# Sparse experts with one token per partition: choices fetched as blocks, value rows added by VectorE

## The chip, the core and the metric

The kernel runs on one core of a Trainium2 chip. Its time is the device time of one execution in microseconds; the time of a kernel is the median of its runs.

## The reference, cut to what matters

One decoder layer for 512 prompt tokens and 32 sample tokens (8 sequences of 4), D = 1024. The change is in its last part, the PEER channel mixer, in which each of 8 heads chooses 16 of 16384 experts for each token:

```python
s = jnp.einsum('tpcd,pckd->tpck', q, peer_keys)          # two halves of 128 keys per head
s1, i1 = lax.top_k(s[:, :, 0], P_TOPK)                   # 16 of 128, twice
s2, i2 = lax.top_k(s[:, :, 1], P_TOPK)
cand = (s1[..., :, None] + s2[..., None, :]).reshape(P_TBLOCK, P_HEADS, P_TOPK * P_TOPK)
cidx = (i1[..., :, None] * P_NKEYS + i2[..., None, :]).reshape(...)
top_s, j = lax.top_k(cand, P_TOPK)
eidx = jnp.take_along_axis(cidx, j, axis=-1)             # 8 x 16 = 128 experts per token
gate = jax.nn.softmax(top_s, axis=-1)
u, v = peer_u[eidx], peer_v[eidx]                        # rows of 1024
act = jax.nn.gelu(jnp.einsum('td,tpkd->tpk', xb, u))
return jnp.einsum('tpk,tpkd->td', gate * act, v)
```

After it `y = layer_norm(DN_ALPHA * h + peer_ffn(h))`.

## The kernel before, in words

Everything ahead of `stage_peer` (projections, mLSTM, attention, merge, first norm) ends near 1087 us and isn't touched. Engines run their own programs and meet at semaphores. In `stage_peer` there are four parts.

- Queries and key scores, 1087 to 1229 us. TensorE projects the queries (L2284) and multiplies them with the keys (`score`, L2191), 4 groups of 4 score blocks for 5 token tiles (4 of 128 prompt tokens, one of 32 samples). ScalarE copies them to `sc`. VectorE ranks them (`top_two`, 16 of 128 per block) and, for every second group, combines two rankings (`choose`, L2444 to L2475) into 16 experts per head.
- The tokens are handled in two ways. The first 384 (tiles 0 to 2, `TD`) are computed densely, against all 16384 experts. The other 160 (tile 3 and the samples, `TG`) are computed sparsely, with their 128 rows of `peer_u` and `peer_v` fetched.
- Hidden stage, 1229 to 1945.6 us. The loop runs over `NCH` = 128 chunks of 128 experts. `hidden(n)` on TensorE is 8 x 2 matmuls of the high part `u_hi` with both parts of h (L2216, L2217) and 8 of the low part `u_lo` (L2227), each over 384 tokens. SyncE loads `u_raw` (4 buffers), ScalarE makes `u_hi` (`high`), and `u_lo` is made by GpSimd (`low`, L2144) up to chunk 47 and from 119, by VectorE (L2517) between. ScalarE applies the gelu, SyncE stores it to HBM. From chunk 47 to 104 the gate tables are made: VectorE writes two one-hots per 4 tokens (`one_hots`, L2483), ScalarE scales one (`scaled`), TensorE multiplies them (`gate_table`, L2247, 96 of them), ScalarE copies the result (`gate_copy`), and SyncE writes it out in 48 pieces of 512 KB.
- Sparse dots lie in the same loop, from chunk 49 to 117. For one token i GpSimd gathers the 128 rows of `peer_u` that it chose (`gather`, L2137; the choices stand in the partitions, a row of 4 KB in each), TensorE copies the token's h to all partitions (`row_spread`, L2203, two matmuls over 512 columns), and VectorE multiplies and sums (`sparse_dot`, L2492). There are 160 of each, six row buffers.
- Output stage, 1945.6 to 2578 us. 32 groups of 4 expert columns. GpSimd loads the value rows of a group (`load_v`, 2 MB, two buffers), SyncE the gate table and the gelus (768 KB each), VectorE multiplies them (`weigh`, L2503), ScalarE makes the high parts (`v_high`, `w_high`), VectorE the low parts (`v_lo` L2508, `w_lo` L2511). `out_tile` (L2270) is 6 matmuls over 512 columns for one column and one of 3 token tiles. After every third column TensorE does `sparse_out` (L2261): 4 tokens' gathered value rows, with the weights as a stationary tile of 32 columns, 40 times in all. Before `load_v(g)` GpSimd issues the gathers of `sparse_rows` in turn. At the end VectorE normalizes the tiles.

The order of the work around the change is written out by hand: `rows_due(n)` and `quads(n)` say what each engine does in chunk n, and each queue is in program order.

Of the kernel before, what the change touches and what calls it, by code (L numbers as in the profile page):

```python
# [8 lines left out]
ALU = mybir.AluOpType  # L9
ACT = mybir.ActivationFunctionType  # L10
AX = mybir.AxisListType
# [1899 lines left out]
def stage_peer(nc, s, io):  # L1911
# [8 lines left out]
    SG = 3  # L1920
    i128 = at("i128", 9136, [P, PK])
# [7 lines left out]
    sc = at("key_scores", 24368, [P, NT, 4 * SG, PK])  # L1929
# [7 lines left out]
    oh = at("oh", 37744, [P, 2, HC * TOPK, TOPK])  # L1937
    chosen = at("chosen", 39792, [P, 3, T])
    picks = [(h0, t) for h0 in range(0, PH, HC) for t in range(NT)]
# [5 lines left out]
    gas = at("gelu_out", 9648, [P, 2, 2, TD])  # L1945
# [8 lines left out]
    row_at = [11184, 12208, 22192, 23216, 49616, 34608]  # L1954
    GR = len(row_at)
    grow = [at(f"gathered{i}", row_at[i], [P, D]) for i in range(GR)]
    hb_at = [7088, 8112, 36656]
    hb_raw = [at(f"h_pair_raw{i}", hb_at[i], [P, D]) for i in range(3)]
    hb = [at(f"h_pair{i}", hb_at[i], [P, D], F32R) for i in range(3)]
    hb_hi = [at(f"h_pair_hi{i}", [49616, 50640, 37680][i], [P, D], F32R) for i in range(3)]  # L1960
    sel = at("pick_row", 13232, [P, 64], F32R)
    wzb = at("sparse_wz", 32560, [P, 4, 4, 64])
    hid = at("sparse_hid", 33584, [P, TG])
    gls = at("sparse_gelu", 33744, [P, TG])
    idx = at("sparse_idx", 33904, [P, TG], U32)
    wsp = at("sparse_w", 34064, [P, TG])
    srow_at = [49616, 12720, 52176, 34608, 5040, 6064, 47568, 48592]
    srow = [at(f"sparse_row{i}", srow_at[i], [P, D]) for i in range(8)]
    hs = at("h_s", 35632, [P, D])
    gb = at("ln2_gb", 7088, [P, 2, D])  # L1970
# [5 lines left out]
    whi = [at(f"w_hi{i}", [50640, 41424][i], [P, GJ, TD], F32R) for i in range(2)]  # L1976
    wlo = [at(f"w_lo{i}", [36656, 42960][i], [P, GJ, TD], F32R) for i in range(2)]
    gin = [at(f"gelu_in{i}", [11184, 44496][i], [P, GJ, TD]) for i in range(2)]
    gt = [at(f"e_gate{i}", [22192, 46032][i], [P, TD, GJ]) for i in range(2)]
    wt = at("e_w", 38704, [P, 2, TD])  # L1980
    hr = at("h2", 944, [P, 4, D])
    st = at("ln2_st", 34232, [P, 2, 6])
    mv = at("ln2_mv", 34248, [P, 2])
    rs = at("ln2_rs", 34256, [P, 2])

    NCH = PK
    E_AT, R_AT, G_AT, G_LEN = 45, 46, 47, 58
    S_AT, S_LEN, HB_AT, HS_AT, SL_AT = 49, 68, 60, 68, 118
    L_AT, W_AT, YS_AT, YP_AT = 119, 121, 26, 122

    due = [S_AT + i * S_LEN / TG for i in range(TG)]
    NSG = TG // 4
    NSS = TS // 4

    def rows_due(n):

        return [i for i in range(TG) if n <= due[i] < n + 1]

    def row_in_group(k, g):

        return P + 4 * k + g if k < NSS else 32 * g + k - NSS

    v_v = io.peer_v.rearrange("(a b) d -> a b d", a=PK)
    sem = Semaphores(nc)
    with ExitStack() as ctx:
# [9 lines left out]
        ul_end = sem("u_low_end")  # L2015
        uh_done, ul_done, ul_late, h_psum, gelu_done = sem("u_high_done"), sem("u_low_done"), sem("u_low_late"), sem("eh_psum"), sem("gelu_done")
# [5 lines left out]
        idx_ready = sem("idx_ready")  # L2022
        row_in = [sem(f"row_in{i}") for i in range(GR)]
        hb_in, hb_split, hb_ready, hb_psum = sem("hb_in"), sem("hb_split"), sem("hb_ready"), sem("hb_psum")
        hid_done, gls_done, wz_zero, sp_read = sem("hid_done"), sem("gls_done"), sem("wz_zero"), sem("sp_read")
        hs_zero, hs_in, gb_in = sem("hs_zero"), sem("hs_in"), sem("ln2_gb_in")
        srow_in = [sem(f"srow_in{i}") for i in range(8)]
        wsp_ready, wzb_ready, sv_psum = sem("wsp_ready"), sem("wzb_ready"), sem("sv_psum")
# [10 lines left out]
        def quads(n):  # L2039
            lo, hi = (min(max((m - G_AT) * NQD // G_LEN, 0), NQD) for m in (n, n + 1))  # L2040
            return range(lo, hi)

        def pieces(n):

            first = [next(m for m in range(NCH) if QD * b + QD - 1 in quads(m)) for b in range(NTB)]
            return [(b, n - first[b]) for b in range(NTB) if 0 <= n - first[b] < NPIECE]

        last_tiles = (3, 0, 1, 2)

        @block.sync  # L2050
        def _(sp):
# [4 lines left out]
            def load_rows(i):  # L2056

                n = 64 if i < 2 else TS
                t0 = TD + 64 * i
                for p0 in range(0, P, n):  # L2060
                    sp.dma_start(hb_raw[i][p0:p0 + n, :], io.h_rows[t0:t0 + n, :]).then_inc(hb_in, 16)

            for n in range(UB):
                load_u(n)
            load_rows(0)
            load_rows(1)
# [4 lines left out]
            for n in range(NCH):  # L2071
# [3 lines left out]
                if n % 2:  # L2075
                    sp.wait_ge(gelu_done, n + 1)
                    c = n % GJ - 1
                    sp.dma_start(io.gelus[n // GJ, :, c * TD:(c + 2) * TD], gas[:, n // 2 % 2, :, :].rearrange("p c t -> p (c t)"))\
                      .then_inc(ga_sent[n // 2 % 2], 16)
                if n == R_AT:  # L2080
                    sp.wait_ge(topk_done, 1)
                    load_rows(2)
# [701 lines left out]
```

## Time and profile before

| | us |
|---|---|
| median of 3 runs | 2606.28 (2597.03 to 2609.4) |
| the profiled execution | 2593.42 |
| its span, first to last instruction | 2591.7 |
| TensorE busy (page, part 1) | 2409.0 (93%) |
| VectorE busy | 1472.6 (57%) |
| ScalarE busy | 897.4 (35%) |
| GpSimd busy | 673.1 (26%) |
| DMA, mean over the span | 200 GB/s |

The page's engines are PE (TensorE matmul), PEld (its weight loads), DVE (VectorE), ACT (ScalarE), POOL (GpSimd) and SP (SyncE). A busy time is an average over stages with different limits, so the rows are read stage by stage. Matmul times in the groups overlap each other, so TensorE's price of a step is read from the chain of waits or from start to start in the timeline.

### The profile page before, as it was taken

How to read it: one execution, taken by the hardware profiler on the slowest of the kernel's cores; microseconds unless marked ns; L12 is line 12 of the kernel's file. 1: busy time of each engine (PE TensorE's matmuls, PEld its weight loads, DVE VectorE, ACT ScalarE, POOL GpSimd, SP SyncE). 2: the span in 40 equal slices, each digit the busy share in tenths (PEclk: the TensorE clock that was granted, in tenths of full speed). 3: DMA queues.
4: the chain of work that ended last, by engine and by line, in shares of the span. 5: the costliest groups of instructions: out<-in, count | busy, mean ns of one | idle time of the engine just before them, and what ended most of it. 6: DMA issues, size and time to landing. Idle time of an engine off the chain costs nothing.

```text
span 2591.7 us, 36634 instructions
## 1 busy us (share of the span) xinstructions
PE 2409.0 (93%) x14200; PEld 2015.6 (78%) x14200; DVE 1472.6 (57%) x3408; ACT 897.4 (35%) x1780; POOL 673.1 (26%) x549
## 2 busy tenths in 40 slices
PE   6999899878977798899999999999999999999997
PEld 6898877765545695488999899999996767777775
DVE  3344332317762332359999888888743454545546
ACT  2122222206841321122333666666332233323321
POOL 0001232211200000100666444444453333233220
PEclk8999999968986699999999999999999999999998
DMA  5234323330012133420555899999989888888881
GB/s 178 80 137 120 108 82 106 119 109 1 1 66 66 50 137 127 150 66 17 165 171 168 275 325 361 354 344 353 374 338 360 315 328 331 327 341 340 322 336 65
DMA packets 160485, 519.25 MB, mean 200 GB/s; under 512 B 15365, under 2 KB 52345, under 8 KB 155577
## 3 DMA queue, kind: packets, MB, share of 16 engines
q1 hardware_dynamic: 104856, 265.27, 30.0%
q0 software_dynamic: 55456, 251.64, 25.9%
q8 instruction: 114, 1.87, 0.3%
q14 instruction: 59, 0.48, 0.1%
HBM read 447.23 MB, written 73.75 MB: 201 GB/s over the span
## 4 chain that ended last, share of the span: by engine, by line
PE 39%; DVE 12%; DMA 3%; issue 3%; POOL 1%; ACT 1%; DVEq 0%; POOLq 0%
PE ps_e L2270 16%; PE ps_e L2216 4%; PE ps_e L2217 4%; PE ps_e L2227 4%; PE ps_e L2247 3%; PE ps_e L2203 3%; PE ps_e L2284 2%; PE ps_e L2261 2%; DMA v_raw<-in_peer_v 2%; DVE oh L2473 2%; DMA u_raw<-in_peer_uT 1%; DVE idx L1898 1%; DVE idx L1902 1%; DVE oh L2468 1%; DVE res L2475 1%
## 5 line engine op out<-in xcount | busy, mean ns | idle before, releaser
L2216 PE MATMUL ps_e<-hTh,u_hi 128*128 128x384 f32 x1024 | 347.2, 339 | 0.0
L2217 PE MATMUL ps_e<-hTl,u_hi 128*128 128x384 f32 x1024 | 346.6, 338 | 0.0
L2508 DVE TENSOR_TENSOR v_lo<-v_raw,v_hi 128x1024 fp32r<-128x1024 f32 x128 | 157.8, 1233 | 292.2 <-ACT v_hi L2349 270.5
L2137 POOL DMA_INDIRECT gathered<-in_peer_u,sparse_idx x160 | 206.5, 1291 | 255.0 <-DVE sparse_hid L2492 238.7
L2137 POOL DMA_INDIRECT sparse_row<-in_peer_v,sparse_idx x160 | 173.1, 1082 | 356.6 <-PE ps_e L2261 312.6
L2270 PE MATMUL ps_e<-v_hi,w_hi 128*128 128x512 f32 x768 | 247.9, 404 | 9.6 <-DVE w_lo L2511 9.6
L2270 PE MATMUL ps_e<-v_lo,w_hi 128*128 128x512 f32 x768 | 242.4, 397 | 0.0
L2349 ACT CAST v_hi<-v_raw 128x1024 fp32r<-128x1024 f32 x128 | 134.4, 1050 | 309.5 <-DMA v_raw<-in_peer_v 309.5
L2270 PE MATMUL ps_e<-v_hi,w_lo 128*128 128x512 f32 x768 | 241.3, 395 | 0.0
L2492 DVE CUSTOM_DVE_ANT_0 gathered<-gathered,ps_e 128x1024 f32<-128x1024 f32 x160 | 193.0, 1218 | 40.2 <-PE ps_e L2203 38.6
L2144 POOL TENSOR_TENSOR u_lo<-u_raw,u_hi 128x1024 fp32r<-128x1024 f32 x57 | 149.2, 2622 | 228.9 <-ACT u_hi L2323 228.9
L2227 PE MATMUL ps_e<-hTh,u_lo 128*128 128x384 f32 x1024 | 200.7, 338 | 0.0
L2270 PEld LDWEIGHTS ps_e<-v_hi,w_hi 128*128 128x128 f32 x768 | 142.0, 189 | 75.2 <-issue 31.9
L2216 PEld LDWEIGHTS ps_e<-hTh,u_hi 128*128 128x128 f32 x1024 | 192.9, 188 | 5.9 <-issue 0.2
L2217 PEld LDWEIGHTS ps_e<-hTl,u_hi 128*128 128x128 f32 x1024 | 192.9, 188 | 5.6
L2227 PEld LDWEIGHTS ps_e<-hTh,u_lo 128*128 128x128 f32 x1024 | 181.8, 188 | 2.0
L238 PE MATMUL ps_proj<-xT_hi,w_hi 128*128 128x256 f32 (+2 forms) x528 | 153.9, 292 | 21.5 <-DVE w_lo L301 13.8
L2270 PEld LDWEIGHTS ps_e<-v_lo,w_hi 128*128 128x128 f32 x768 | 145.6, 190 | 35.0
L2270 PEld LDWEIGHTS ps_e<-v_hi,w_lo 128*128 128x128 f32 x768 | 145.1, 189 | 34.5
L2323 ACT CAST u_hi<-u_raw 128x1024 fp32r<-128x1024 f32 x128 | 134.4, 1050 | 73.7 <-DMA u_raw<-in_peer_uT 73.6
L239 PE MATMUL ps_proj<-xT_lo,w_hi 128*128 128x256 f32 (+2 forms) x528 | 154.2, 292 | 0.0
L240 PE MATMUL ps_proj<-xT_hi,w_lo 128*128 128x256 f32 (+2 forms) x528 | 153.8, 291 | 0.0
(477 smaller groups left out, 4827.3 us busy)
## 6 DMA issues: line engine op xcount, KB each, us to landing
u_raw<-in_peer_uT SPq DMA_DIRECT2D x128, 512.0 KB
v_raw<-in_peer_v POOLq DMA_DIRECT2D x32, 2048.0 KB
hidden_gelu<-gelu_out SPq DMA_DIRECT2D x64, 384.0 KB
gate_tables<-g_buf SPq DMA_DIRECT2D x48, 512.0 KB
e_gate<-gate_tables SPq DMA_DIRECT2D x32, 768.0 KB
gelu_in<-hidden_gelu SPq DMA_DIRECT2D x32, 768.0 KB
w_raw<-in_w_tiles SPq DMA_DIRECT2D x45, 512.0 KB, 3.6
gw_raw<-in_merge_tiles SPq DMA_DIRECT2D x16, 512.0 KB, 4.7
```

The lines of the kernel that those rows point to most:

```text
L238: pe.matmul(out, hi, s.xTh[:, dc, toks], start=(dc == 0), stop=False)
L239: pe.matmul(out, hi, s.xTl[:, dc, toks], start=False, stop=False)
L240: last = pe.matmul(out, lo, s.xTh[:, dc, toks], start=False, stop=(dc == DC - 1))
L2137: pool.indirect_dma_start(out=row, out_offset=None, in_=table, in_offset=bass.IndirectOffsetOnAxis(ap=idx[:, column:column + 1], axis=0))\
L2144: pool.tensor_tensor(u_lo[:, n % UB, :, :], u_raw[:, n % UB, :, :], u_hi[:, n % UB, :, :].bitcast(F32), ALU.subtract).then_inc(done, 1)
L2216: pe.matmul(ps[:, n % 2, 0:TD], u_hi[:, n % UB, dc, :], hTh[:, dc, :], start=(dc == 0), stop=False)
L2217: pe.matmul(ps[:, n % 2, 0:TD], u_hi[:, n % UB, dc, :], hTl[:, dc, :], start=False, stop=False)
L2227: last = pe.matmul(ps[:, n % 2, 0:TD], u_lo[:, n % UB, dc, :], hTh[:, dc, :], start=False, stop=(dc == DC - 1))
L2270: last = pe.matmul(ps[:, 2 * t + half, :], w[u][:, c, ts], v[u][:, c, half * 512:(half + 1) * 512], start=(g == 0 and c == 0 and w is whi ...
L2323: act.copy(u_hi[:, n % UB, :, :], u_raw[:, n % UB, :, :]).then_inc(uh_done, 1)
L2492: dve.tensor_tensor_reduce(out=row, in0=row, in1=ps[:, 6 - 2 * (i % 2):8 - 2 * (i % 2), :], scale=1.0, scalar=0.0, op0=ALU.mult, op1=ALU.a ...
L2508: dve.tensor_tensor(v_lo[g % 2][:, c, :], v_raw[g % 2][:, c, :], v_hi[g % 2][:, c, :].bitcast(F32), ALU.subtract).then_inc(vl_done, 1)
```

## The change

Sparse tokens move from "a choice in each partition, one token after another" to "a token in each partition, one choice after another".

- One gather now fetches, for each of the 128 tokens of tile 3, the row of its c-th choice: 128 blocks. The samples are packed: 32 tokens x 4 groups of 2 heads fill the partitions, 32 choices each: 32 blocks. Again 160 gathers of `peer_u` and 160 of `peer_v`.
- h of tile 3 and of the packed samples is copied once to PSUM (banks 4, 5 and 6, 7), and the dot reads it there. `row_spread`, the split of h for it and `pick_row` go.
- The value rows are added by VectorE, `acc = row * weight + acc`, one instruction of 1024 elements per gather, in SBUF (`y3`) for tile 3 and in PSUM for the samples, which TensorE folds at the end (`fold_pack`, two matmuls). `sparse_out` and its weight tiles go.
- VectorE's order: tile 3, the packed samples and tile 0 are ranked and chosen before chunk 29; tiles 1 and 2 have their second half (two rankings, two choices each) between chunks 30 and 64. Gate tables: 16 in chunks 31 to 52 (tile 0, first half), 80 from chunk 66 to 108.
- Row dots: 14 before chunk 29, one per chunk from 30 to 64, 111 from 65 to 118. Seven value rows from chunk 121, 153 in columns 0 to 117 of the output stage.
- All 128 `low(n)` are on GpSimd.
- `weigh`, `w_high` and `w_lo` work on a group of 4 columns at once, with the column as the innermost index; `out_tile` reads its stationary tile with a stride of 4. The gelus are stored by group (32 stores of 768 KB).
- Scores go through two PSUM banks instead of four.

The diff, cut to its core:

```diff
+    quad_at = [31 + q * 22 // QD for q in range(QD)] + [66 + (q - QD) * 43 // (NQD - QD) for q in range(QD, NQD)]
+    PRE = 14
+    row_due = ([0] * PRE + [30 + i for i in range(35)] + [65 + i * 54 / (U_END - 49) for i in range(U_END - 49)]
+               + [121 + i for i in range(7)] + [NCH + i * 118 / (ALL - U_END - 7) for i in range(ALL - U_END - 7)])
...
@@ block.gpsimd
-            for n in range(G_AT + 1):
-                low(n, ul_done)
-            pool.wait_ge(idx_ready, 1)
-            for i in range(TG):
-                if i >= GR:
-                    pool.wait_ge(hid_done, i - GR + 1)
-                gather(io.peer_u, grow[i % GR][:, :], i, row_in[i % GR])
...
-            k = 2
-            for g in range(2, NG):
-                while k < NSG and 3 * k - 4 <= GJ * (g - 1):
-                    sparse_rows(k)
-                    k += 1
-                pool.wait_ge(o_psum, GJ * (g - 1))
-                load_v(g)
+            low(0)
+            low(1)
+            for i in range(8):
+                gather(i)
+            for n in range(2, NCH):
+                low(n)
+                if 4 <= n < 4 + PRE - 8:
+                    gather(n + 4)
+                for i in rows_due(n + 1):
+                    gather(i)
+                if n == W_AT - 2:
+                    for g in range(2):
+                        pool.wait_ge(g_sent[1 - g], 16 * NPIECE * (NTB // 2))
+                        load_v(g)
+            for n in range(NCH):
+                for i in rows_due(NCH + n + 1):
+                    gather(i)
+                if n % GJ == GJ - 1 and n // GJ + 2 < NG:
+                    pool.wait_ge(o_psum, n + 1)
+                    load_v(n // GJ + 2)
...
@@ block.tensor
-                    if dc % 4 == 0 and dc // 4 < len(spread):
-                        row_spread(spread[dc // 4])
...
-                        if n % 3 == 1 and n // 3 < NSG:
-                            sparse_out(n // 3)
...
@@ block.vector
+            def use_row(i):
+                tile, landed, turn = row_place(i)
+                row, c = tile[:, :].rearrange("p (a b) -> p a b", a=2), column(i)
+                dve.wait_ge(landed, 16 * (turn + 1))
+                if i < U_END:
+                    bank = 4 if c < NS3 else 6
...
+                    dve.tensor_tensor_reduce(out=row, in0=row, in1=ps[:, bank:bank + 2, :], scale=1.0, scalar=0.0, op0=ALU.mult,
+                                             op1=ALU.add, accum_out=hid[:, c:c + 1]).then_inc(rows_done, 1)
+                    return
+                dve.wait_ge(rows_done, i)
+                acc = ps[:, 6:8, :] if c >= NS3 else y3[:, :].rearrange("p (a b) -> p a b", a=2)
...
+                    dve.scalar_tensor_tensor(out=acc, in0=row, scalar=wsp[:, c:c + 1], in1=acc, op0=ALU.mult, op1=ALU.add)\
+                       .then_inc(rows_done, 1)
...
+            for n in range(NCH):
+                g, c = n // GJ, n % GJ
+                spread = rows_due(NCH + n)
+                if g:
+                    if c == 0:
+                        weigh(g)
+                    if c == 0:
+                        for i in spread[:1]:
+                            use_row(i)
+                        spread = spread[1:]
+                        w_low(g)
+                    v_low(g, c)
+                for i in spread:
+                    use_row(i)
```

`gather(i)` waits, from the fifth row on, for the row that had its buffer before (`rows_done`); there are five, then six buffers.

## Rows read from the trace of the kernel before

**Rows 1.** By stretch: length, PE, PEld, DVE, ACT, POOL busy, clock, DMA share, GB/s.

```profile
1229.00:1429.00 200.00, 198.25 (x1129) 197.94 (x1128) 193.03 (x663) 70.33 (x100) 121.30 (x46) 1.00 0.57 168
...
1550.00:1850.00 300.00, 299.38 (x1842) 290.40 (x1841) 259.68 (x394) 187.59 (x432) 138.68 (x106) 1.00 0.98 351
...
1945.60:2578.00 632.40, 622.84 (x2945) 449.13 (x2943) 321.87 (x447) 184.63 (x254) 185.87 (x186) 0.99 0.81 312
```

**Rows 2.** The chain of waits: start us, us, what.

```profile
1656.65 1.41 PE ps_e L2227 x8
1658.06 1.78 PE ps_e L2247 x16
...
2268.67 1.85 PE ps_e L2261 x16
2270.52 12.79 PE ps_e L2270 x54
```

**Rows 3.** The timeline of TensorE in one chunk.

```profile
1600.51 0.62 PE L2203 MATMUL ps_e<-h_pair,pick_row 128*128 128x512 f32 x2
...
1600.98 0.34 PE L2216 MATMUL ps_e<-hTh,u_hi 128*128 128x384 f32 x1
```

**Rows 4.** VectorE: ends of two choices (chain), start of one (timeline).

```profile
1373.74 2.30 DVE res L2475
...
1381.96 0.22 DVE L2444 TENSOR_TENSOR cand<-top 128x64 f32<-128x64 f32 x1
...
1400.48 2.30 DVE res L2475
```

**Rows 5.** Groups by line and shape: count, busy us, mean ns, idle before and releasers.

```profile
L2492 DVE CUSTOM_DVE_ANT_0 gathered<-gathered,ps_e 128x1024 f32<-128x1024 f32 x160 | 193.0, 1218 | 40.2 <-PE ps_e L2203 38.6 <-issue 1.7
...
L2508 DVE TENSOR_TENSOR v_lo<-v_raw,v_hi 128x1024 fp32r<-128x1024 f32 x128 | 157.8, 1233 | 292.2 <-ACT v_hi L2349 270.5 <-issue 21.7
...
L2483 DVE TENSOR_TENSOR one_a<-i,chosen 128x512 f32<-128x512 f32 x96 | 66.0, 688 | 17.1 <-PE ps_e L2247 9.7 <-issue 6.1
```

**Rows 6.** The timelines of GpSimd and VectorE while both work.

```profile
1361.39 2.46 POOL L2144 TENSOR_TENSOR u_lo<-u_raw,u_hi 128x1024 fp32r<-128x1024 f32 x1 [1.80 <-ACT u_hi L2323]
...
1361.62 2.31 DVE L2462 SCALAR_TENSOR_TENSOR partf<-placef 128x64 f32<-128x64 f32 x1
```

**Rows 7.** Busy time by stretch, ten us without gate pieces.

```profile
1870.00:1880.00 10.00, 8.10 (x44) 7.79 (x45) 8.43 (x13) 2.89 (x4) 4.91 (x5) 1.00 1.04 414
```

**Rows 8.** GpSimd's timeline, and the software queue from 2093 and 2103: packets, MB, share.

```profile
2087.76 0.57 POOL L2133 DMA_DIRECT2D v_raw<-in_peer_v  x1 [1.91 <-PE ps_e L2270]
...
2093.80 0.97 POOL L2137 DMA_INDIRECT sparse_row<-in_peer_v,sparse_idx  x1 [5.47 <-PE ps_e L2261]
...
2095.07 0.94 POOL L2137 DMA_INDIRECT sparse_row<-in_peer_v,sparse_idx  x1 [0.30 <-issue]
...
q0 software_dynamic: 41, 0.67, 88.1%
...
q0 software_dynamic: 197, 0.70, 86.1%
```

**Rows 9.** Timelines of the last value loads, and the chain's last load.

```profile
2515.68 0.32 SPq L2109 DMA_DIRECT2D e_gate<-gate_tables  x1
...
2517.47 0.57 POOL L2133 DMA_DIRECT2D v_raw<-in_peer_v  x1 [8.08 <-PE ps_e L2270]
...
2526.89 1.05 ACT L2349 CAST v_hi<-v_raw 128x1024 fp32r<-128x1024 f32 x1 [10.68 <-DMA v_raw<-in_peer_v]
...
2538.36 7.77 DMA v_raw<-in_peer_v
```

**Rows 10.** TensorE's timeline after a wait, and the stretch that follows.

```profile
2559.50 0.94 PE L2270 MATMUL ps_e<-v_hi,w_hi 128*128 128x512 f32 x2 [4.66 <-DVE w_lo L2511]
...
2560.00:2570.00 10.00, 10.00 (x38) 7.92 (x37) 2.91 (x6) 0.00 (x0) 0.00 (x0) 0.84 0.01 2
```

**Rows 11.** The groups by line, TensorE's weight loads.

```profile
L2270 PEld LDWEIGHTS ps_e<-v_hi,w_hi 128*128 128x128 f32 x768 | 142.0, 189 | 75.2 <-issue 31.9 <-DVE w_lo L2511 13.4
```

More of the change, by code:

```diff
@@ L2003, in stage_peer, with row_place @@
+    def row_place(i):
+        return (early[i % 5], early_in[i % 5], i // 5) if i < EARLY else \
+            (later[(i - EARLY) % 6], later_in[(i - EARLY) % 6], (i - EARLY) // 6)
     v_v = io.peer_v.rearrange("(a b) d -> a b d", a=PK)
@@ L2273, in out_tile, with fold_pack @@
                 return last
+            def fold_pack():
+                pe.wait_ge(fold_ready, 1)
+                pe.wait_ge(yp_ready, 1)
+                for half in range(2):
+                    last = pe.matmul(ps[0:TS, 6 + half, :], fold[:, :], yp[:, half * 512:(half + 1) * 512], start=True, stop=True)
+                last.then_inc(f_psum, 1)
             pe.wait_ge(keys_in, 16)
@@ new lines, in _ @@
+            link(dve.tensor_tensor(fold[:, :], fold[:, :], s.ident[:, 2 * TS:3 * TS], ALU.add))
+            dve.tensor_tensor(fold[:, :], fold[:, :], s.ident[:, 3 * TS:P], ALU.add).then_inc(fold_ready, 1)
+            dve.wait_ge(iotas, 2)
+            for t in (3, 0, 1, 2):
+                rank(0, t)
+                dve.sem_inc(sc_free, 1)
+            rank(1, 3)
+            choose(0, 3, HC)
+            row_numbers(0, 3, slice(0, HC))
+            rank(1, 0)
+            choose(0, 0, HC)
@@ new lines, in _ @@
+            for i in range(0, 3):
+                use_row(i)
+            rank(1, 1)
+            for i in range(3, 5):
+                use_row(i)
+            rank(1, 2)
+            for i in range(5, 8):
+                use_row(i)
+            rank(2, 3)
+            rank(3, 3)
+            choose(HC, 3, HC)
+            row_numbers(HALF3, 3, slice(HC, PH))
+            below_top(3, PH)
+            for i in range(8, 11):
+                use_row(i)
+            rank_pack()
+            choose(0, PACK, HP)
@@ new lines, in _ @@
+            row_numbers(NS3, PACK, slice(0, HP))
+            below_top(PACK, HP)
+            rank(2, 0)
+            rank(3, 0)
+            for i in range(11, PRE):
+                use_row(i)
+            choose(HC, 0, HC)
+            below_top(0, PH)
+            shares(0, 3, PH, gsp[:, 0:NS3].rearrange("p (h k) -> p h k", h=PH))
+            shares(1, PACK, HP, gsp[:, NS3:NSL].rearrange("p (h k) -> p h k", h=HP))
+            shares(2, 0, PH, res[:, 0, 0, :, :])
+            for n in range(R_AT[0], NCH):
+                ahead, spread = quads(n), rows_due(n)
+                if n == 31:
+                    dve.wait_ge(r_done, 1)
@@ new lines, in _ @@
+                    use_row(i)
+                for t in (1, 2):
+                    if n == R_AT[0] + 14 * (t - 1):
+                        choose(0, t, HC)
+                    if n == R_AT[0] + 14 * (t - 1) + 5:
+                        rank(2, t)
+                    if n == R_AT[0] + 14 * (t - 1) + 7:
+                        rank(3, t)
+                    if n == R_AT[0] + 14 * (t - 1) + 9:
+                        choose(HC, t, HC)
+                        below_top(t, PH)
+                if n == E_AT[1]:
+                    dve.wait_ge(chain, step.n)
+                    dve.sem_inc(topk_done, 1)
+                    shares(3, 1, PH, res[:, 1, 0, :, :])
+                    shares(4, 2, PH, res[:, 2, 0, :, :])
```

684 lines of the change are left out of this document (317 added, 367 removed).

## The prediction

> **What bounds the kernel now.** Read the stretches first. The expert mixer runs from 1229 to 2578 us in two stages: 128 chunks that make the hidden activations (`hidden(n)`, to 1945.6) and 32 groups of four expert columns that add the value rows (`out_tile`). In the stretches shown TensorE is busy for 98.5 to 100% of the time, so its instruction count sets both stages [rows 1]. But from 1550 to 1850 the DMA engines stand at 0.98 of their time as well, at 351 GB/s; both limits lie on each other there. In the output stage the DMA share is 0.81.
>
> Then the chain of waits gives TensorE's prices. Eight hidden matmuls cost 1.41 us, so a chunk of 24 costs 4.23. Two gate tables cost 1.78, so one costs 0.89. Three output columns cost 12.79, so one costs 4.26 and a group of four 17.0. One `sparse_out` costs 1.85 [rows 2]. The timeline gives `row_spread`: the next matmul starts 0.47 us after the pair does [rows 3].
>
> The hidden stage is then 128 x 4.23 = 541, 96 x 0.89 = 85 and 160 x 0.47 = 75, together 701 of its 716.6 us, 15 us being waits. The output stage is 128 x 4.26 = 545 and 40 x 1.85 = 74, together 619 of 632.4, with 13 us of waits.
>
> **What leaves TensorE.** `row_spread` (75 us) and `sparse_out` (74 us) go; both were on the path. Two fold matmuls and fewer transposes are below 2 us. If nothing else became late, the stages would be 626 and 545 plus the old waits, 149 us less.
>
> **Hidden stage, chunks 0 to 29.** VectorE must rank and choose tile 3, the packed samples and tile 0 before chunk 29. Before, 20 rankings and 10 choices end near 1429, one period after the choice whose last step is at 1400.48 [rows 4]. Now 13 rankings and some 4.5 choices come first, at the prices below 155 us less, and 14 row dots more, 18 us: it is done near 1292, and chunk 29 ends at 1356. TensorE sets this part: 30 x 4.23 = 127 us. The 14 early gathers meet a DMA share of 0.57 [rows 1] and cost nothing; without that cover each is 1.3 us of traffic.
>
> **Chunks 30 to 64.** TensorE needs 35 x 4.23 + 16 x 0.89 = 162. VectorE now has here what it did before chunk 45: four rankings and four choices for tiles 1 and 2. Ranking and choice come every 26.7 us, and a choice alone takes from 1381.96 to 1402.8, so 20.8 and 5.9 [rows 4]. With 35 row dots at 1.22 + 0.08 and 16 pairs of one-hots at 2 x 0.69 [rows 5] plus 0.5 of waiting for GpSimd it has 107 + 46 + 30 = 183 us. It can't be spread: `scaled(q)` stands ahead of `gelu(n)` on ScalarE, TensorE waits for the one-hots, and VectorE can be only two tables ahead. Up to chunk 52, where the last of these tables is, VectorE has 183 - 20.8 - 12 x 1.3 = 147 against TensorE's 23 x 4.23 + 14 = 111; the last choice is hidden by chunks without tables. I take 36 us of waiting plus a few for the lumps: 204, bounds 162 and 225.
>
> The 0.5 is a wait for a port: a 128x64 operation of two SBUF inputs that starts while GpSimd subtracts takes 2.31 us and ends with it [rows 6]. All 128 `low(n)` at 2.4 us are on GpSimd now, where 71 were on VectorE.
>
> **Chunks 65 to 118.** TensorE needs 54 x 4.23 + 80 x 0.89 = 300. The traffic: 54 x 0.524 MB of u, 111 gathers of 0.524, 40 gate pieces of 0.524 and 13 of 0.786 of gelus make 118 MB. At the 351 GB/s of [rows 1] that is 336 us, at the 414 that the same queues reached without gate pieces [rows 7] 284, so TensorE would be first. GpSimd has 2.4 + 2.06 x (0.97 + 0.3) = 5.0 us per chunk and VectorE 2.06 x 1.3 + 1.5 x 1.9 = 5.5, both near TensorE's 5.6. The mix is that of [rows 1], so I take 330, bounds 300 and 365. The last nine chunks are 38 us and 8 of waits for the first value loads. The stage is 127 + 204 + 330 + 46 = 707, which is 10 less than before: nearly all of the 75 us goes to VectorE's choices and to the DMA queues.
>
> **Output stage.** Per group VectorE has 4 `v_low` at 1.23, two operations of 1536 elements at about 1.78 (by the step from 0.69 to 1.23 for 512 more [rows 5]) and 5.2 rows at 1.3: 15.2 of 17.0 us. That would fit. What doesn't is the order. At the end of a group GpSimd issues `load_v(g+2)` (2 MB), and the gathers for columns 1 to 4 of the next group come behind it, in the same queue. VectorE does its work in order: the row of column 1 stands ahead of `v_low` of column 2. So column 2 waits for that row, and the row for the load.
>
> That the row waits for the load is in the trace: a load was issued at 2087.76 and a gather at 2093.80, the next 1.27 us later; until 2095 the software queue moved 41 packets for 0.67 MB, 16 KB each as only the load has, and at 2103 to 2105 197 packets for 0.70 MB, the 4 KB of gathers [rows 8]. The load itself takes 7.8 us alone (from 2538.36, 7.77 until it is there) and 9.4 with gate and gelu tables issued 1.8 us ahead of it (2517.47 to 2526.89) [rows 9]. In the new order the tables are issued some 2 us ahead, so 9.4.
>
> The period of a group: 0.3 to issue, 9.4 to land, 1.5 for the gather behind it (0.524 MB at the 0.35 MB/us of [rows 8]), 1.3 for the dot-sized row add, 0.45 for the second row that three columns in ten have, 1.23 for `v_low`, and then two columns, 8.5: 22.7 us, where TensorE needs 17.0. Rows are due up to column 118, so 29 groups are stretched: 29 x 5.7 = 165. The stage is 545 + 13 + 165 = 723, 91 more than before. With a load of 7.8 it is 29 x 4.1 = 119, so 677. An addition on top: after 4.7 us of TensorE idleness the granted clock was 0.84 over ten us, which is 1.2 GHz for three of them [rows 10]; at most 1.6 us per group, 46 us, which I leave to the range.
>
> The Trainium skill, DMA: Bandwidth & Descriptors, Latency and other measured facts, has this very shape, 128 partitions of 16 KiB at a pitch of 512 KiB, at 207 GB/s (from another queue), so 10.1 us as an estimate; the trace has 7.8 alone and 9.4 beside other traffic, and the measurement decides. By the Trainium skill's figure the stage would be about 20 us longer.
>
> **Other edits.** Scores use two PSUM banks instead of four; a tile takes TensorE longer than the copy of 512 elements takes ScalarE, so nothing to 5 us. `w` is now read with a stride of four elements as the stationary tile; no row shows such a read, the nearest, the packed one, is hidden below the matmul, so nothing, and at worst one more load time of 0.19 on each of 2304 matmuls [rows 11]. The end is the same three tiles.
>
> **The sum.** The profiled execution took 2593.4 (span 2591.7). -10 + 91 = +81 gives 2674. The median of the unprofiled runs lies 12.9 higher, so 2687.
>
> **The rivals.** (1) TensorE's saving counts. For it: both stages are TensorE-bound in [rows 1]. It needs that the row adds don't hold up `v_low`, and that the DMA engines give 400 GB/s or more: 650 to 690 and 560 to 600, so 2470 to 2550 on the median's scale. Against it are [rows 8]. The Trainium skill, DMA: Bandwidth & Descriptors, Queues, rings and completion order, says the same of one queue: an engine takes its descriptors in ring order and turns only between queues; by that rule, the trace agrees. (2) The hidden stage gains (chunks 65 to 118 at 300, few stalls: -50) and the load lands in 7.8 (+45): 2600, no change. (3) The port and the DMA queues make the hidden stage longer too, 750, and the clock falls in each stretched group: 2687 + 43 + 30 = 2760. It decides where GpSimd and VectorE together exceed TensorE's 5.6 us per chunk. (4) The strided read is slow: 2304 x 0.19 = 438 less what hides, about +250. That the change doesn't do what it says (a step of the old way left in) is not open: both TensorE steps are gone from the code.
>
> **How the numbers follow.** Forecast 0.57, its own range 2630 to 2740 by the bounds above; rival 1 0.16, rival 2 0.12, rival 3 0.12, rival 4 0.03. The range 2550 to 2760 leaves out rivals 1 and 4, 19 in 100. Faster by over 0.5% (about what a measurement of this kernel can tell from no change) is rival 1 and a third of 2 and a little of the forecast: 0.22; within 0.5% 0.06; slower 0.72.
>
> **What would show it.** Output stage: TensorE idle before column 2 of each group, waiting for `v_lo`, with VectorE's row add waiting for its gather; a period near 22.7 us; a lower DMA share than 0.81. Right or wrong by those alone. Hidden stage: TensorE waiting for `one_b` in chunks 31 to 52, and ScalarE's `u_hi` for the DMA later. If the period is 17 to 18, the gathers don't wait for the load and rival 1 holds. If `u_lo` on GpSimd is what TensorE waits for, rival 3.

## The result, and the profile after

| | before | after |
|---|---|---|
| median of 4 runs, same chip (us) | 2605.42 (2597.03 to 2609.4) | 2701.53 (2694.36 to 2711.08) |
| profiled execution, span | 2591.7 | 2692.7 |
| up to the hidden stage | 1229.0 | 1229.6 |
| hidden stage | 716.6 | 719.4 |
| output stage, to the last matmul | 632.4 | 729.8 |
| end | 13.7 | 13.9 |
| TensorE busy | 2409.0 | 2336.5 |

The changed kernel is slower: 1.0376 times the time before, interval 1.0334 to 1.0417, where 2687 us was forecast. 149 us of matmuls left TensorE, as forecast, but it is busy for only 72 us less, since what stays takes it longer (below), and the kernel takes 96 us longer. Nearly all of that is in the output stage.

First the stretches of the kernel after, cut as the prediction cuts them: chunks 0 to 29, 30 to 64, 65 to 118, the last nine, the output stage. The columns are those of [rows 1].

```profile
1229.60:1356.60 127.00, 127.00 (x725) 127.00 (x724) 87.23 (x262) 54.99 (x62) 84.83 (x38) 1.00 0.58 193
1356.60:1556.90 200.30, 168.77 (x972) 167.48 (x971) 159.26 (x441) 95.57 (x156) 121.58 (x69) 0.92 0.67 236
1556.90:1904.60 347.70, 314.28 (x1966) 309.17 (x1965) 280.99 (x390) 241.20 (x516) 262.93 (x166) 0.98 0.93 341
1904.60:1949.00 44.40, 35.99 (x193) 35.72 (x194) 20.78 (x14) 18.95 (x23) 30.70 (x17) 0.92 0.84 316
1949.00:2678.80 729.80, 607.90 (x2308) 571.83 (x2307) 457.29 (x376) 167.60 (x162) 173.21 (x182) 0.92 0.69 270
```

In the output stage of before TensorE was busy for 98.5% of the time, at a clock of 0.99 and with a DMA share of 0.81 [rows 1]. Now it is 83%, 0.92 and 0.69: no resource is full, which is what a chain of waits leaves. The chain of the kernel after shows one turn per group (start, us, what):

```profile
2196.68 8.89 PE ps_e L2231 x36
2205.58 0.29 issue
2205.86 0.57 POOL v_raw L2130
2206.43 0.30 issue
2206.74 9.29 DMA row<-in_peer_v,sparse_idx
2216.03 0.02 issue
2216.06 1.28 DVE y L2530
2217.34 1.15 DVE v_lo L2553
2218.49 0.04 issue
2218.53 9.02 PE ps_e L2231 x36
```

Two columns (`ps_e`), the issue of the load (`v_raw`), the gather's row, the row add (`y`), the low part of column 2 (`v_lo`), two columns: those are the links that the prediction named. The load issues from 1995.79 to 2644.28 lie 28 groups apart, 23.2 us each; 22.7 was forecast. What answers to [rows 8] is the software queue, from 2210 to 2212 and from 2214 to 2216 us:

```profile
q0 software_dynamic: 57, 0.93, 111.8%
...
q0 software_dynamic: 216, 0.82, 102.1%
```

57 packets of 16 KB first, which only the load has, then 216 packets of about 4 KB, the gathers. And what answers to [rows 5] and [rows 11], groups of the page:

```profile
L2231 PE MATMUL ps_e<-v_hi,w_hi 128*128 128x512 f32 x768 | 272.2, 438 | 121.9 <-DVE v_lo L2553 121.8
L2231 PEld LDWEIGHTS ps_e<-v_hi,w_hi 128*128 128x128 f32 x768 | 213.7, 313 | 143.3 <-DVE v_lo L2553 95.4
L2530 DVE SCALAR_TENSOR_TENSOR y<-row,sparse_w,y 128x1024 f32<-128x1024 f32 x128 | 164.1, 1282 | 208.9 <-DMA row<-in_peer_v,sparse_idx 206.5
L2303 ACT ACTIVATE gelu_out<-ps_e 128x384 f32<-128x384 f32 x128 | 110.9, 866 | 145.7 <-PE ps_e L2206 144.0
```

TensorE waits 122 us for `v_lo` (one wait of 10.3 at the start of the stage, then 44 of 0.3 to 5.1, up to two per group), VectorE 207 us for the rows of tile 3 and 45 for those of the samples. A weight load takes 313 ns where it took 189 [rows 11].

The waits cost more than their own length, because behind most of them the granted clock is lower for a while. Two stretches of 4.6 us behind a wait of 2.24 us that ended at 2207.80 (columns as above):

```profile
2207.80:2212.40 4.60, 4.60 (x13) 3.89 (x14) 0.99 (x1) 0.72 (x1) 3.51 (x4) 0.63 1.02 413
2212.40:2217.00 4.60, 4.60 (x21) 4.60 (x20) 0.94 (x1) 0.00 (x0) 0.94 (x1) 1.00 0.99 404
```

13 matmuls against 21 in the same time, at a mean clock of 0.63, so mostly at 1.2 GHz. Here that fell into columns 0 and 1, beside the load. Of the 27 two-column pieces that lie on the chain, 8 took 8.9 to 9.0 us and the rest 10.1 to 11.4; the mean is 10.2. TensorE is busy in this stage for 608 us; in kernel 6 below, with the same matmuls and weight loads and hardly a wait, for 553.

### The profile page after: what moved, and what is told of

Read it like the earlier page. It is cut to its first block, busy times and chain, and to the rows that moved or that the text cites. A ratio compares the mean times of both kernels' runs of the same rounds, so it can differ in the third digit from the quotient of the medians.

```text
span 2692.7 us, 33900 instructions
## 1 busy us (share of the span) xinstructions
PE 2336.5 (87%) x13238; PEld 2091.2 (78%) x13238; DVE 1539.4 (57%) x3102; ACT 917.7 (34%) x1682; POOL 811.4 (30%) x620
## 4 chain that ended last, share of the span: by engine, by line
PE 31%; DMA 12%; DVE 10%; issue 2%; ACT 2%; POOL 2%; SPq 0%; DVEq 0%; POOLq 0%; ACTq 0%
PE ps_e L2231 11%; DMA row<-in_peer_v,sparse_idx 9%; PE ps_e L2253 4%; PE ps_e L2202 4%; PE ps_e L2203 4%; PE ps_e L2206 4%; PE ps_e L2223 2%; DMA u_raw<-in_peer_uT 2%; DVE one_b L2507 2%; DVE y L2530 1%; DVE one_a L2507 1%; DVE v_lo L2553 1%; DVE row L2522 1%; ACT one_b L2310 1%; PE ps_e L2191 1%
## 5 line engine op out<-in xcount | busy, mean ns | idle before, releaser
L2156 POOL TENSOR_TENSOR u_lo<-u_raw,u_hi 128x1024 fp32r<-128x1024 f32 x128 | 322.2, 2517 | 206.6 <-ACT u_hi L2296 205.4
L2231 PEld LDWEIGHTS ps_e<-v_hi,w_hi 128*128 128x128 f32 x768 | 213.7, 313 | 143.3 <-DVE v_lo L2553 95.4
L2530 DVE SCALAR_TENSOR_TENSOR y<-row,sparse_w,y 128x1024 f32<-128x1024 f32 x128 | 164.1, 1282 | 208.9 <-DMA row<-in_peer_v,sparse_idx 206.5
L2341 ACT CAST w_hi<-e_w 128x1536 fp32r<-128x1536 f32 x32 | 47.4, 1480 | 536.4 <-DVE e_w L2544 536.4
L2231 PEld LDWEIGHTS ps_e<-v_lo,w_hi 128*128 128x128 f32 x768 | 214.8, 312 | 7.1
L2231 PEld LDWEIGHTS ps_e<-v_hi,w_lo 128*128 128x128 f32 x768 | 213.8, 311 | 6.5
L2522 DVE CUSTOM_DVE_ANT_0 row<-row,ps_e 128x1024 f32<-128x1024 f32 x150 | 180.7, 1213 | 52.8 <-DMA row<-in_peer_u,sparse_idx 52.5
L2149 POOL DMA_INDIRECT row<-in_peer_v,sparse_idx x160 | 166.9, 1043 | 48.9 <-issue 48.4
L2149 POOL DMA_INDIRECT row<-in_peer_u,sparse_idx x150 | 165.8, 1105 | 41.9 <-issue 18.1
L2303 ACT ACTIVATE gelu_out<-ps_e 128x384 f32<-128x384 f32 x128 | 110.9, 866 | 145.7 <-PE ps_e L2206 144.0
```

The source lines that it names most:

```text
L2149: pool.indirect_dma_start(out=row[:, :], out_offset=None, in_=io.peer_u if i < U_END else io.peer_v, in_offset=bass.IndirectOffsetOnAxis(a ...
L2156: pool.tensor_tensor(u_lo[:, n % UB, :, :], u_raw[:, n % UB, :, :], u_hi[:, n % UB, :, :].bitcast(F32), ALU.subtract).then_inc(ul_done, 1)
L2231: last = pe.matmul(ps[:, 2 * t + half, :], w[u][:, ts, c], v[u][:, c, half * 512:(half + 1) * 512], start=(g == 0 and c == 0 and w is whi ...
L2303: act.activation(gas[:, g % 2, :, c], ps[:, n % 2, 0:TD], ACT.Gelu).then_inc(gelu_done, 1)
L2522: dve.tensor_tensor_reduce(out=row, in0=row, in1=ps[:, bank:bank + 2, :], scale=1.0, scalar=0.0, op0=ALU.mult, op1=ALU.add, accum_out=hid[ ...
L2530: dve.scalar_tensor_tensor(out=acc, in0=row, scalar=wsp[:, c:c + 1], in1=acc, op0=ALU.mult, op1=ALU.add)\
```

## The experiments

All start from the changed kernel. Ratios are to the kernel before, run beside each (its medians were 2598 to 2605 us), with their 95% interval, so kernels are compared by ratios; half an interval is 4 to 14 us. The table gives the profiled execution in stretches: end of chunk 29 to end of 64, to 118, to 127, and from there to the end (output stage and the last tiles), by the starts of the gelus.

| kernel | median us | ratio | 30-64 | 65-118 | 119-127 | rest |
|---|---|---|---|---|---|---|
| the kernel before | 2605.4 | 1 | 202 | 353 | 35 | 646 |
| the changed kernel | 2701.5 | 1.0376 (1.0334-1.0417) | 200 | 348 | 44 | 744 |
| 1 gathers three ahead | 2565.2 | 0.9881 (0.9865-0.9898) | 203 | 346 | 45 | 613 |
| 2 low parts first | 2556.9 | 0.9843 (0.9825-0.9862) | 200 | 346 | 45 | 610 |
| 3 packed weights | 2713.6 | 1.0456 (1.0438-1.0474) | 200 | 344 | 45 | 757 |
| 4 earlier start | 2703.7 | 1.0415 (1.0394-1.0436) | 180 | 346 | 45 | 757 |
| 5 load in SyncE's queue | 2691.6 | 1.0345 (1.0296-1.0394) | 200 | 345 | 44 | 748 |
| 6 both links | 2531.0 | 0.9734 (0.9693-0.9775) | 201 | 348 | 46 | 573 |
| 7 both links, packed | 2520.3 | 0.9693 (0.9652-0.9734) | 203 | 348 | 45 | 570 |
| 8 order of choices | 2681.1 | 1.0289 (1.0238-1.0339) | 170 | 346 | 45 | 759 |
| 9 half rows | 2703.6 | 1.0391 (1.0346-1.0437) | 203 | 340 | 45 | 759 |
| 10 no low part | 2688.9 | 1.0320 (1.0265-1.0374) | 202 | 323 | 45 | 752 |
| 11 6 and 8 together | 2493.5 | 0.9587 (0.9547-0.9627) | 170 | 344 | 44 | 577 |
| 12 11, low part split | 2511.5 | 0.9655 (0.9617-0.9693) | 170 | 361 | 45 | 576 |

One execution has its own scatter. Where no edit touches chunks 65 to 118 (kernels 1 to 8 and 11), they take 344 to 348 us. Where none touches the output stage (4, 8, 9 and 10), the rest takes 752 to 759, and the changed kernel's 744 comes from the fastest of its four runs. The hidden stage starts anywhere from 1225 to 1238 us, in work that no edit touches. Differences of that size are no effect of an edit.

### The two links of the output stage (1, 2, 6)

1, the gathers go ahead of the load:

```diff
             for n in range(NCH):
-                for i in rows_due(NCH + n + 1):
-                    gather(i)
+                for m in (range(n + 3, n + 4) if n else range(1, 4)):
+                    for i in rows_due(NCH + m):
+                        gather(i)
```

> The changed kernel with one edit: in the output stage GpSimd issues each gather three columns ahead instead of one, so those of columns 1 and 2 of the next group go into the queue before the load of the value rows. Theory (the gathers stand behind the load in their queue, the row add behind the gather, the low part of column 2 behind the row add): the wait per group goes, the stage falls from 730 us to what TensorE needs, 128 columns at 4.26 to 4.45 and some 15 of waits, 560 to 585, and the time from 2701 to 2530 to 2560. Rival a (VectorE has too much work in this stage): no change, 2690 to 2710. Rival b (the 2.2 us that TensorE waits before column 0, for w, are a chain of their own): they stay, 32 x 2.2 = 70 us, 2600 to 2630.

2565: 129 us less than the changed kernel by the ratios, just above the theory's range. Rival a falls, since VectorE does the same work in 613 us as in 744, and so does rival b, by the time and by the waits that are left (14 of them, 33 us).

2, VectorE's order, with the gathers as they were:

```diff
-                spread = rows_due(NCH + n)
+                spread = rows_due(NCH + n - 2) if n >= 2 else []
```

> The changed kernel with the other link cut: gathers and load keep their order in the queue, but VectorE uses the rows of a column only after the low part of the column two further on. Theory: the gather still lands some 10 us after the load is issued, but TensorE's columns 0 to 3 need 17 us and none of their low parts stands behind that row: TensorE's waits go as in the first experiment, 2530 to 2570. Rival a (VectorE has too much work, or the load itself is what comes late): no change, 2690 to 2710. If only this one gains and not the first, the row adds are late for another reason than the queue.

2557, in the theory's range. The chain of this kernel shows the row as late as in the changed kernel:

```profile
2178.41 0.57 POOL v_raw L2130
2178.99 0.30 issue
2179.29 11.31 DMA row<-in_peer_v,sparse_idx
...
2191.82 1.76 DVE e_w L2544
2193.61 1.49 ACT w_hi L2341
2195.12 0.98 DVE w_lo L2548
...
2196.80 1.23 DVE v_lo L2553
...
2198.16 17.63 PE ps_e L2231 x72
```

The row's 11.3 us are still there, but now what hangs on them is the first column of the next group, some 19 us on. So cutting either link alone takes most of the wait away: it needs the late row and the order behind it. What TensorE still waits for `v_lo` is 33 us in both kernels (from 1965 us on; 121 in the changed one). Kernel 1 moves the gathers ahead of two things, the load and GpSimd's own wait for the end of the group, so it doesn't tell which of them makes the row late. 6 cuts both (gathers two columns ahead, rows used two columns late):

> The changed kernel with both links of the output stage cut: gathers two columns ahead, and the rows of a column used after the low part of the column two further on. In the run with the second link alone TensorE still waited 33 us in all at the first column of a group, because VectorE came to the weights of the next group only after the row behind the load. Theory: that row is no longer behind the load, so these waits fall to below 10 and the time from 2557 to 2525 to 2540. Rival (VectorE's own work for the first column, weights, a row, high and low part, some 9 us in a chain, is what comes late): no change against 2557. Column price: 4.33 to 4.41 us if the strided read costs TensorE something at full clock, 4.26 if not.

2531, in the theory's range; waits are 6.7 us, and one piece of its chain is 1494 matmuls long. The output stage of 6 by stretch, and what TensorE waited for in it (us in total, times, longest):

```profile
1955.60:2514.90 559.30, 552.65 (x2308) 549.24 (x2307) 453.94 (x375) 168.36 (x162) 227.97 (x179) 1.00 0.88 350
```

```profile
PE ps_e L2232 <- DVE v_lo L2554: 6.7, 3, 5.1
```

559 us at full clock, so rival 1 of the prediction (560 to 600) is what this stage gives once the links are cut.

### Which property of the load delays the row (5)

GpSimd issues no load from group 2 on; SyncE does, at the same point. GpSimd's wait for the end of the group stays ahead of its gathers:

```diff
+            def load_v(g):
+                sp.wait_ge(o_psum, GJ * (g - 1))
+                sp.dma_start(v_raw[g % 2][:, :, :], v_v[:, g * GJ:(g + 1) * GJ, :]).then_inc(vs_in[g % 2], 16)
```

> The changed kernel with the loads of the value rows for groups 2 to 31 issued by SyncE in its own hardware queue, at the same point (the end of a group). GpSimd still waits for the end of the group before the next gathers, and VectorE's order stays; so only the queue of the load is another. Theory (a gather stands behind the load because both are in one queue): now it only shares the engines with it, 0.52 MB at half of 350 GB/s are 3 us, plus the 1.5 it takes alone, so the row is there 4 to 6 us after the load is issued instead of 10, before TensorE has done its two columns: 2560 to 2600. Rival (it is the DMA engines' bandwidth after the end of a group, whatever the queue): the row comes at 9 to 10 us again, 2690 to 2710.

2692, the rival's number, and the theory falls; the intervals of 5 and of the changed kernel overlap. From 2200 to 2202 and from 2204 to 2206 us of this kernel (packets, MB, share):

```profile
q1 hardware_dynamic: 118, 0.95, 113.0%
...
q1 hardware_dynamic: 41, 0.67, 78.3%
q0 software_dynamic: 40, 0.16, 19.9%
```

The row is there 9.6 us after the gather's issue (2198.35 to 2207.99), and that time has two halves. For the first 4.6 us the gather's queue (q0) moves no packet at all; over the 28 groups it is 4.2 to 5.2 us. A gather of the same kernel that was issued at 1469.41, with no value load beside it, began after 1.6 and was through after 4. Why the start is late with the load in another queue stays open. From then on the two queues share the engines by turns of one packet each, 41 against 40, and a packet of the load has 16 KB where the gather's has 4, so the gathers get a fifth of the traffic and not half. The Trainium skill, DMA: Bandwidth & Descriptors, Queues, rings and completion order, says that an engine goes round between its queues packet by packet, which agrees with these counts; that packets of different size make that an unequal share is what this run adds. It accounts for the second half of the 9.6 us, not for the first.

### The strided weights (3, 7)

```diff
-    wt = at("e_w", 38192, [P, 2, TD, GJ])
+    wt = at("e_w", 38192, [P, 2, GJ, TD])
...
-                        last = pe.matmul(ps[:, 2 * t + half, :], w[u][:, ts, c], ...
+                        last = pe.matmul(ps[:, 2 * t + half, :], w[u][:, c, ts], ...
```

> The changed kernel with the weights of a group laid out column after column (the product is written with a stride, its high and low part and the stationary tile are read packed). Weight loads fall from 312 ns to about 190 in either theory. Theory (the strided read is hidden below the matmuls, and only the slower clock after a wait makes two columns cost 8.9 instead of 8.5): no change, 2690 to 2710. Rival (the strided read costs TensorE 0.18 us per column): 128 x 0.18 = 23 us less, 2678. Rival 4 of the prediction (one load time of 0.12 in the open on each of 2304 matmuls): 2425 or so, and that can't be, since the stage would have shown it.

2714, no gain, and by the ratios 0.8% longer. TensorE waits 143 us for `v_lo` instead of 122. Two groups of its page suggest why:

```profile
L2231 PEld LDWEIGHTS ps_e<-v_lo,w_hi 128*128 128x128 f32 x765 | 155.3, 203 | 38.7
L2544 DVE TENSOR_TENSOR e_w<-gelu_in,e_gate 128x1536 f32<-128x1536 f32 x31 | 91.2, 2943 | 0.0
```

Weight loads are at 203 ns, but the product, now written with a stride, takes 2.94 us instead of 1.75 and stands in VectorE's order ahead of column 0. That this is the whole of the 0.8% is argued, not shown. The same edit on kernel 6:

> Both links of the output stage cut, as in the run at 2531, and the weights laid out packed. There TensorE ran without waits at 4.29 us per column, with 310 ns per weight load. Theory (the strided read is hidden but for a few ns): weight loads 190 to 205 ns, a column 4.25 to 4.27, so 128 x 0.03 = 4 us less in TensorE, and VectorE's 32 products of 2.9 us instead of 1.75 stay hidden: 2525 to 2532. Rival (the strided write, 38 us more on VectorE in this stage, shows): 2535 to 2560.

2520. The intervals of 6 and 7 overlap, so the chain says more: in kernel 7 1368 matmuls take 320.50 us, 4.217 per column, against 355.74 for 1494, 4.286, in kernel 6, at a granted clock of 0.99 and 1.00. The strided read costs 0.07 us per column, 9 us in all. Rival 4 of the prediction (250 us) falls: the 120 ns lie below the matmuls.

### The hidden stage (4, 8, 9, 10, 12)

4 moves the first gate tables, the exponentials and the choices seven chunks ahead (`E_AT, R_AT = (22, 64), (23, 65)`).

> The changed kernel with the gate tables of tile 0, the exponentials ahead of them and VectorE's rankings and choices for tiles 1 and 2 begun seven chunks earlier (chunk 22 and 23 instead of 29 and 30), the 35 rows spread over 42 chunks. Theory (chunks 30 to 64 are set by VectorE, 200 us where TensorE needs 162, and VectorE stood idle for 36 us before chunk 30, waiting for the exponential): 25 to 35 us less, 2666 to 2676. Rival a (what is gained there is lost to the DMA engines from chunk 65 on, since they run at 0.96): no change. Rival b (these waits are the one-hots' own, wherever they stand): no change.

2704: rival b. Counted from the start of the stage chunk 29 ends after 149 us instead of 127, and chunk 64 after 329 instead of 327: nothing is gained. Over the whole stage TensorE waits 50.7 us for `one_b`, against 57.3, and for the tables of tile 0 alone 27, against 29. VectorE's idle time only moved, from before the tables to behind them: it is busy for 27 of the 76 us from 1480 to 1556 in this kernel.

8 keeps the chunk and changes the order: `choose(0, 1, HC)`, `rank(2, 1)` and `rank(3, 1)` stand ahead of the wait for the exponential, and

```diff
-    quad_at = [31 + q * 22 // QD for q in range(QD)] + ...
+    quad_at = [31, 32, 33, 34, 40, 41, 42, 43, 49, 50, 51, 52, 58, 59, 60, 61] + ...
```

> The changed kernel with another order in VectorE's part of the hidden stage. The first choice and the two rankings of tile 1 come ahead of the wait for the exponential, where VectorE stood idle for 36 us; the 16 gate tables of tile 0 stand in four bunches of four (chunks 31 to 34, 40 to 43, 49 to 52, 58 to 61) with the remaining choices between the bunches; the second exponential comes one chunk earlier. Theory, after the earlier start gained nothing: TensorE loses 30 us of waits and some 6 of slow clock there because a choice of 21 us stands ahead of one-hots that are needed within 13, not because VectorE has too much to do in total. Then most of that goes: chunks 30 to 64 fall from 200 to 165 to 175 and the time from 2701 to 2665 to 2680. Rival (the DMA engines from chunk 65 take it back, because four pieces of gates now fall among the gathers): chunk 127 ends where it did, 2695 to 2710.

Chunks 30 to 64 fall from 200 to 170 us, as the theory says, and TensorE's wait for `one_b` in them from 29 us to 4. With all engines' work the same in sum, chunk 127 comes 31 us sooner after the start of the stage. By the ratios 23 us arrive in the time (0.0087 x 2600), with intervals of 11 to 13 us on either side of each, so the two agree. In 11, where the output stage's waits are gone, the same order gives 38 us against 6, by the ratios.

What kernel 8 doesn't separate: it places the choices between the bunches, and it also takes 33 us of VectorE's work (a choice of 20.8 us and two rankings of 5.9) out of this stretch, to where VectorE was idle. The prediction's own count up to the last table, 147 us for VectorE against 111 for TensorE, would lose most of its gap by the second alone. No run does one of the two alone.

9 halves the bytes of 111 gathers. 10 takes all but 16 columns of GpSimd's subtraction away in the same chunks, and TensorE uses the high part a second time instead. Neither computes the layer any more:

```diff
+                if 49 <= i < U_END:
+                    pool.indirect_dma_start(out=row[:, 0:D // 2], out_offset=None, in_=io.peer_u.rearrange("n (a d) -> (n a) d", a=2), ...
...
+                if 65 <= n < 119:
+                    pool.tensor_tensor(u_lo[:, n % UB, 0, 0:16], u_raw[:, n % UB, 0, 0:16], ...
```

> The changed kernel with gathers of half a row (2 KB instead of 4) for the 111 rows of chunks 65 to 118; the row dots run over the whole buffer as before, so their result is wrong, and every engine's work is the same. Traffic of these chunks falls from 118 to 89 MB, at 350 GB/s 254 us, below TensorE's 300. Theory (the DMA engines set these chunks, 348 us): 305 to 315, and the time from 2701 to 2660 to 2670. Rival (GpSimd and VectorE, lengthened by each other at their port, set them): 340 to 350 and 2690 to 2705.

> The changed kernel without the low part of u in chunks 65 to 118: GpSimd subtracts 16 columns instead of 1024, and TensorE uses the high part a second time in its place, so that the output is wrong and TensorE's work and the traffic are the same. GpSimd is rid of 54 x 2.5 = 135 us there. Theory (DMA engines set these chunks): 340 to 350 us for them, 2690 to 2705 in all; one-hots fall from 903 and 1051 ns towards 690 all the same, which shows what the port costs VectorE. Rival 3 of the prediction (port and GpSimd set them): 305 to 320, 2660 to 2675. If both this and the one with half rows gain, both limits lie close together.

9 changes nothing in the time (chunks 65 to 118 in 340 us, where the kernels with these chunks untouched have 344 to 348). 10 takes 21 to 25 us off them (323); its ratio is 15 us lower, within the intervals. The chunks of 9 by stretch:

```profile
1559.20:1899.60 340.40, 312.77 (x1952) 308.44 (x1951) 281.18 (x390) 240.72 (x515) 260.83 (x165) 0.98 0.79 263
```

The one-hots in these chunks, first in the changed kernel:

```profile
L2507 DVE TENSOR_TENSOR one_b<-i,chosen 128x512 f32<-128x512 f32 x80 | 85.5, 1069 | 0.0
L2507 DVE TENSOR_TENSOR one_a<-i,chosen 128x512 f32<-128x512 f32 x80 | 74.2, 928 | 34.6 <-PE ps_e L2223 34.6
```

and in kernel 10:

```profile
L2511 DVE TENSOR_TENSOR one_b<-i,chosen 128x512 f32<-128x512 f32 x80 | 55.2, 691 | 0.0
L2511 DVE TENSOR_TENSOR one_a<-i,chosen 128x512 f32<-128x512 f32 x80 | 55.2, 690 | 60.4 <-PE ps_e L2227 42.7 <-issue 17.6
```

With a DMA share of 0.79 instead of 0.93 the chunks are 4 to 8 us shorter: the DMA engines don't set them. Without GpSimd's subtraction the one-hots are back at the 690 ns of [rows 5], and TensorE's wait for `one_b` falls from 28.3 to 7.3 us. So the link is GpSimd's subtraction beside VectorE's one-hots, which fits the port of [rows 6], and from there ScalarE and TensorE. The gathers come no sooner in kernel 10: VectorE waits 27 us for their rows in these chunks, against 29. Below 323 us the DMA engines may be next: in 10 their share is 0.98, at 367 GB/s.

11 is 6 and 8 together, 12 gives every third low part of chunks 66 to 107 to VectorE on top.

> Both links of the output stage cut, as in the run at 2531, and the order of choices of the run at 2681 together. Theory (hidden and output stage are limited apart from each other, so their gains add): the order of choices takes the 20 to 30 us off that it took off the changed kernel, 2500 to 2512. Rival (what the hidden stage gains is lost again at its end, because the value rows of the output stage or its first loads come no earlier): 2520 to 2535.

> The same, and between chunks 66 and 107 every third low part of u is made by VectorE instead of GpSimd (14 x 1.23 us more for VectorE, 14 x 2.5 less for GpSimd). The run without the low part showed that GpSimd's subtraction and the port it holds cost the chunks 65 to 118 some 25 us. Theory (GpSimd's share counts in proportion): a third of 25 less, minus VectorE's 17 us of extra work as far as it shows: 0 to 10 us below the kernel without it. Rival (VectorE's one-hots are the link whatever delays them, so its own extra work costs as much as the port did): 5 to 15 us above it.

11 is the best kernel of the study, 2493.5 us, 4% below the kernel before and some 7 below the theory's range. 12 is 18 us above it, the rival's sign and a little more than its range. The chunks 65 to 118 take 361 us instead of 344. GpSimd's subtractions that are left take 2731 ns on average (2584 in 11), one-hots 1024 and 835 (846 and 1123 in 11), and TensorE waits 9 us more for `one_b`. The low parts on VectorE cost at least what they save at the port.

## Why the prediction was right, point by point

**The sum.** +81 us was forecast, +101 is the difference of the profiled executions and +96 that of the medians. The hidden stage gave +3 instead of -10, the output stage +97 instead of +91. By chunks the hidden stage lost 9 us in the last nine and gained 1 and 5 in the two stretches before, against the same chunks of the kernel before.

**Chunks 0 to 29** took 127.0 us, as forecast. VectorE was done at 1326 and not near 1292 (it is idle from there to 1362); that step was 34 us off, its cause stays open, and it cost nothing, as TensorE sets this part.

**Chunks 30 to 64** took 200 us, forecast 204. The size was right, and so was the place: TensorE waits 29 us there for `one_b`. That VectorE's work can't be spread was wrong: kernel 8 spreads it, with the same work in sum, and takes 170. Kernel 4 shows that an earlier start alone gives nothing. Whether the distance between a choice of 21 us and the next one-hots costs the 30 us, or the amount that VectorE has up to the last table, is not separated.

**Chunks 65 to 118** took 348 us, forecast 330, bounds 300 and 365. The step that failed is the one that put them on the DMA engines: by kernel 9 the traffic is worth 4 to 8 us, by kernel 10 the subtraction on GpSimd 21 to 25. This was rival 3's mechanism, which the prediction weighed only for the case that the stage reached 750, and not by the sign given for it: TensorE waits 0.3 us for `u_lo`, the cost comes by the one-hots. The sign given for the DMA engines, ScalarE's `u_hi` waiting for the DMA, came true (28 us) and meant nothing for the time: in kernel 10 that wait is 43 us and the chunks are shorter.

**The output stage.** The chain was forecast link by link and is there link by link. Its terms were off in both directions. Load and gather: forecast 0.3 + 9.4 + 1.5 = 11.2 us, measured 0.29 + 0.57 + 0.30 + 8.9 (mean of the row's piece in 27 groups) = 10.1. Row adds and `v_low`: forecast 3.0, measured 2.8. Two columns: forecast 8.5, measured 10.2. Of the difference 1.3 is the slow clock (10.2 against the 8.9 of the pieces at full clock), 36 us in 28 groups, and 0.3 the start behind a wait (8.9 against twice 4.286). The prediction had left the clock to the range with at most 46. So the number is near partly by luck: load, gather and row adds came out 1.3 us shorter per group than forecast, the two columns 1.7 longer.

The 207 GB/s that the prediction took from the Trainium skill, DMA: Bandwidth & Descriptors, Latency and other measured facts, and set beside its 9.4 us, are for copies between tensors in HBM. The load here goes to SBUF, and alone it took 7.72 us (from 2644.28).

**What was shown and what not.** That order, not an engine's load, costs the 97 us is shown by kernels 1, 2 and 6. That it is the common queue is not: kernel 5 takes it away and gains nothing. What the runs agree with is that the row is late when it is issued behind or beside a load of 2 MB in 16 KB packets, in whichever queue. No run leaves the load out, and none frees the gathers of GpSimd's wait alone, so how much of the 9 us is the load and how much the gather's own time isn't measured. The Trainium skill's rule on ring order (DMA: Bandwidth & Descriptors, Queues, rings and completion order), which the prediction set beside [rows 8], agrees with the changed kernel's packets, but a kernel rewritten by that rule alone would not have been faster.

**The rivals.** 1 asked that the row adds don't hold up `v_low`, and they did. Its other condition, 400 GB/s, was not needed: the output stage of kernel 6 ran at 350. 2 asked for a gain in the hidden stage, which is there only with another order. 4 is measured at 9 us. Most of TensorE's 149 us do count once little else is late: kernel 11 is 107 us below the kernel before.

## What to carry to other kernels

When a step moves from one engine to an idle one, follow the order on the new engine: what stands behind the new instruction, and what that instruction waits for, can cost more than its own length. Prefetch small gathers ahead of a large load, or put work that doesn't need them first; giving the load another queue didn't help here, with packets four times the size. Where one engine alternates between long blocks and short work that others need soon, move the blocks to where nobody waits. A wait that a forecast names as a sign can come true and still not set the time; a run that takes its cause away tells.

## What was not expected of the hardware

- Three engines were slower on 4-byte elements with a stride: a weight load read with a stride of 16 bytes takes 313 ns instead of 189, ScalarE's gelu of 384 elements written with a stride of 16 bytes 866 ns instead of 488 (the mean of that group in the profile of before), VectorE's product of 1536 elements written with a stride of 1536 bytes 2943 ns instead of 1752. The Trainium skill, SBUF — State Buffer, Door 1: The DMA port swizzle, has lines of 16 bytes in SBUF and a penalty for each access that crosses to a new one; all three cross with every element, and these rows show a price of 1.66 to 1.77 times.
- Two queues at the DMA engines took turns by packet whatever its size: 41 packets with 0.67 MB beside 40 with 0.16 MB (kernel 5).
- A wait of TensorE of only 2.24 us was followed by a fall of the granted clock; the prediction's only row of that had 4.66 [rows 10]. The length of the last wait alone doesn't tell: behind waits of 2.38 and 2.27 us, before 2240.89 and 2264.71, two columns took 8.89 and 9.03 us, so at full clock.
